# GpSimd's two sample-state transfers and its zeroes wait for four input units of block 1 instead of the last unit of block 0

## The chip, the cores and the metric

The kernel runs as one program on one core of a Trainium2 chip. The metric is the device time of one execution in microseconds (us), lower is better. Five queues of instructions run side by side: TensorE (PE in the rows; PEld is its weight load), VectorE (DVE), ScalarE (ACT), GpSimd (POOL) and SyncE (SP). Each takes its own instructions strictly in order, and they meet at counting semaphores. DMA engines move data; SyncE, ScalarE and GpSimd issue the transfers.

## The reference, cut to what matters

One inference step of a two-layer decoder, for a prompt of 512 tokens and for 8 samples of one token each, 520 tokens together (`TOK`), 1024 features. Layer 0 (block 0) is sparse attention, layer 1 (block 1) a sliding window of 128 keys; each is followed by an MLP with squared ReLU, and each half by a layer norm:

```python
for i in range(DEPTH):                       # DEPTH = 2
    m_p, ... = mixer_a_prompt / mixer_b_prompt (y_p, ...)
    m_s, ... = mixer_a_sample / mixer_b_sample (y_s, ...)
    y_p = post_norm(y_p, m_p, ...);  y_s = post_norm(y_s, m_s, ...)
    y_p = post_norm(y_p, squared_relu_mlp(y_p, w1, w2), ...)   # y_s alike
```

The part that the change touches is the window mixer of the samples. Its keys and values are a stored state of 128 tokens with the new token appended, and the last 128 of them are also outputs:

```python
keys = jnp.concatenate([win_k, k], axis=1)
vals = jnp.concatenate([win_v, v], axis=1)
...
return out @ w_out, keys[:, -wb:], vals[:, -wb:]
```

## The kernel before, in words

**Units.** Every dense product is cut into units: a 1024x128 block of weights (512 KB in `WRAW`) against all 520 tokens. A unit is 48 matmuls of 128x260: 8 contraction tiles, two token halves (`g`), and three products, because weights and activations are each split into a high and a low part. Units are counted over the whole program: block 1's input projection is units `B_IN` = 86 to 95, its output projection 96 to 103, then its MLP. `unit_done` counts finished units.

For each unit SyncE loads the raw weights (L432), ScalarE makes the high part (L1069 or L1019, `hi_done`), VectorE the low part as raw minus high (L1494 or L1419, `lo_dve`), and TensorE multiplies. There are two raw buffers, so the load of unit u+2 waits for VectorE's low part of unit u.

**End of block 0.** The last units of the MLP (`last_units`) run in halves of 260 tokens, and the layer norm of one half runs on VectorE and ScalarE while TensorE works on the other. VectorE writes the new activations `X32` by `even` (L1582) and their low parts `XL` (L1592). TensorE then takes the first four input units of block 1, 86 to 89, together in `first_quad` (matmuls on L606): half g=0 of all four in four steps of two tiles as `XL` comes, then `stats` for the other half, then half g=1. Unit 86 is counted only with its g=1 part, so `unit_done` reaches 90 when all of `first_quad` is done.

**Input projection.** Behind `first_quad` TensorE runs units 90 and 91, five transposes, and units 92 to 95 (`input_units(3, 5)`, L576). VectorE's program there, in order, is:

```python
low_parts(2, 3)                    # low parts of units 92, 93
dve.wait_ge(ev_act, A_OUT + 1)
dve.wait_ge(win_in, 32)
V.tensor_copy(KW[:, :, P:P + 1], ...)      # L2014
low_parts(3, 5)                    # low parts of units 94 to 97
```

TensorE begins unit 94 only with VectorE's low part of unit 94.

**GpSimd's part.** `KW` (keys, 128 partitions x 8 samples x 129) and `VW` (values, 127 rows x 8 samples x 128) receive the stored state. GpSimd waits for `unit_done`, issues the `KW` transfer (L555) and the `VW` transfer (L556), each of which adds 16 to `win_in`, clears `QB` (L559, `z_qb`), waits for the new values in `NAT` (`vt_ev`), and issues eight row transfers into `VW` (L562, `vwin_in`). `KW` and `QB` lie over `HL`, the low part of the MLP's hidden layer, which TensorE reads up to unit 85. The readers are: the copy on L2014 (`win_in`); the copies into `QB` on L2022 (`z_qb`) ahead of the attention; and TensorE inside block 1's attention (L988, L998).

Of the kernel before, what the change touches and what calls it, by code (L numbers as in the profile page):

```python
# [48 lines left out]
A_IN, A_OUT, MLP0, B_IN, B_OUT, MLP1, U_END = 0, 14, 22, 86, 96, 104, 168  # L49
# [124 lines left out]
def program(nc, io):  # L174
    with ExitStack() as ctx:
# [14 lines left out]
        def sem(name):  # L190
            return ctx.enter_context(nc.semaphore(name))
# [131 lines left out]
        unit_done = sem("unit_done")  # L323
# [59 lines left out]
        def load_page(eng, n, pg):  # L383

            fetch_page(eng, n, pg, page_number(eng, n, pg))

        def load_index_page(eng, half, c, pg, done):


            page = eng.value_load(PT[0:1, bass.ds(c * 16 + (8 * half + pg), 1)],  # L390
                                  min_val=0, max_val=POOL_PAGES - 1)
            eng.dma_start(IK[HD * half:HD * half + HD, bass.ds(c, 1), pg * P:(pg + 1) * P],  # L392
                          io["cacheI"][bass.ds(page, 1), :, :].rearrange("o d k -> d o k")
                          ).then_inc(done, 16)

        def page_numbers(eng, q, samples):

            return {n: [page_number(eng, n, pg) for pg in range(*kv_pages(n)[q])]
                    for n in samples}
# [6 lines left out]
        def load_values(eng, q, numbers):  # L406

            eng.wait_ge(unit_done, A_OUT)
            for n in V_LATE:
                if kv_before(n):  # L410
                    eng.wait_ge(kv_used, kv_before(n))
                load_sample(eng, q, n, numbers)
# [103 lines left out]
        @block.gpsimd  # L516
        def _(pool):
            nc.gpsimd.memset(NAT[:, 4, :], 0.0).then_inc(z_nat, 1)
            nc.gpsimd.memset(QB[:], 0.0).then_inc(z_qb, 1)
            pool.wait_ge(pt_in, 16)  # L520
            for half in range(2):
                with pool.Fori(0, 4 - half * IDX_SP) as c:
                    for pg in range(NPG):
                        load_index_page(pool, half, c, pg, idx_in)

            def low_part(u, slot):
                pool.wait_ge(hi_done, u + 1)
                nc.gpsimd.tensor_tensor(WLO[:, slot], WRAW[:, slot], WHI[:, slot].bitcast(F32),
                                        ALU.subtract).then_inc(lo_pool, 1)


            for n in (6, 7):
                with pool.Fori(0, NPG) as pg:
                    load_page(pool, n, pg)
            numbers = page_numbers(pool, 1, V_LATE)
            pool.wait_ge(ds_mm, 3)
            nc.gpsimd.memset(QB[:], 0.0).then_inc(z_qb, 1)
            with pool.Fori(0, 4) as pg:
                load_page(pool, 3, pg)
            for u in range(POOL_LO[0], A_OUT):  # L540
                low_part(u, u % 2)
                if u < POOL_LO[0] + 4:
                    load_page(pool, 3, 4 + u - POOL_LO[0])
            load_values(pool, 1, numbers)
            for u in range(A_OUT, POOL_LO[1]):
                low_part(u, u % 2)

            pool.wait_ge(ev_dve, 16)
            for h in range(NH):
                nc.gpsimd.tensor_tensor(BT[:, h, 256:512], BT[:, h, 256:512],  # L550
                                        CST[:, C_WIN:C_WIN + 2 * P], ALU.add
                                        ).then_inc(bwin, 1)

            pool.wait_ge(unit_done, B_IN)
            pool.dma_start(KW[:, :, 0:P], io["swk"]).then_inc(win_in, 16)  # L555
            pool.dma_start(VW[0:P - 1, :, :],  # L556
                           io["swv"][:, 1:P, :].rearrange("b k d -> k b d")
                           ).then_inc(win_in, 16)
            nc.gpsimd.memset(QB[:, 0:DB * 144], 0.0).then_inc(z_qb, 1)  # L559
            pool.wait_ge(vt_ev, 5)  # L560
            for b in range(DB):
                pool.dma_start(VW[P - 1:P, b, :], NAT[b:b + 1, 4, 0:P]  # L562
                               ).then_inc(vwin_in, 16)
# [1568 lines left out]
```

## Time and profile before

| | us |
|---|---|
| median of 3 runs | 1273.05 (1267.76 to 1275.14) |
| the profiled execution | 1270.1 |
| its span, first to last instruction | 1268.4 |
| TensorE busy | 1206.0 (95%) |
| VectorE busy | 708.6 (56%) |
| ScalarE busy | 473.9 (37%) |
| GpSimd busy | 94.8 (7%) |

Times below are microseconds from the start of the span. A timeline row is: start, duration, engine, line, operation, written tile <- read tiles, shape, and in brackets the idle time of the engine just before it with what ended it. TensorE's matmuls are pipelined: one has a duration of 0.28 us, but one starts every 0.12 us. The granted clock is TensorE's, as a share of full speed (2.4 GHz). The time that a transfer takes to land is counted from the start of its issue. The change touches the stretch from 690 to 780.

### The profile page before, as it was taken

Reading aid. Unit: us, or ns where it says so; the run is one execution under the profiler, and the core shown is the slowest. Engines: PE = TensorE matmul, PEld = TensorE weight load, DVE = VectorE, ACT = ScalarE, POOL = GpSimd, SP = SyncE. Lnnn points to the kernel's source line nnn. Section 1 sums busy time; section 2 is a strip of 40 time slices with the busy share of each in tenths; the row PEclk is TensorE's granted clock in tenths of the full one; section 3 lists DMA queues with packets and bytes.
Section 4 is the critical chain, followed back from the end, with each engine's and each line's share of the span. In section 5 each row is a group of like instructions: output and inputs, shape, how many; then the busy total and the mean of one; then the engine's idle time right before and its main releaser. Section 6 shows DMA issues by size and latency. Waiting matters only on the chain.

```text
span 1268.4 us, 25585 instructions
## 1 busy us (share of the span) xinstructions
PE 1206.0 (95%) x9574; PEld 1108.6 (87%) x9574; DVE 708.6 (56%) x1443; ACT 473.9 (37%) x865; POOL 94.8 (7%) x129
## 2 busy tenths in 40 slices
PE   8998979999999999999999897899999999999995
PEld 4958745589999999999999895599999999999995
DVE  2288989857843433433467627867633433433477
ACT  2342147744522331322334337834522322322332
POOL 4334300100040000000000210000000000000000
PEclk9999979999999999999999997999999999999998
DMA  6687570233122222222233221031222222222221
GB/s 202 192 282 242 182 240 16 75 111 103 48 91 92 96 86 97 86 93 89 93 110 114 50 93 48 1 101 67 67 84 100 83 100 83 98 84 98 84 84 68
DMA packets 62091, 131.04 MB, mean 103 GB/s; under 512 B 9739, under 2 KB 34483, under 8 KB 61890
## 3 DMA queue, kind: packets, MB, share of 16 engines
q1 hardware_dynamic: 44114, 112.94, 26.8%
q10 hardware_dynamic: 12096, 9.44, 2.4%
q0 software_dynamic: 5808, 7.67, 2.1%
q8 instruction: 48, 0.79, 0.3%
q14 instruction: 25, 0.20, 0.1%
HBM read 125.41 MB, written 9.79 MB: 107 GB/s over the span
## 4 chain that ended last, share of the span: by engine, by line
PE 72%; DVE 13%; issue 6%; POOLq 3%; ACT 2%; POOL 2%; SPq 1%; DMA 1%; ACTq 0%; DVEq 0%
PE PS L576 60%; PE PS L606 6%; DVE PB L1712 2%; DVE YA L1576 2%; PE PS L756 1%; PE PS L743 1%; DVE PB L1737 1%; SPq L379 1%; DVE YA L1563 1%; POOLq L370 1%; PE PS L770 1%; DVE X L1582 1%; DVE RSTD L1568 1%; POOL IK L392 1%; POOLq L390 1%
## 5 line engine op out<-in xcount | busy, mean ns | idle before, releaser
L1419 DVE TENSOR_TENSOR WLO<-WRAW,WHI 128x1024 fp32r<-128x1024 f32 x118 | 145.3, 1232 | 354.6 <-ACT WHI L1019 354.5
L1019 ACT ACTIVATE WHI<-WRAW 128x1024 fp32r<-128x1024 f32 x126 | 133.5, 1059 | 384.7 <-PE PS L576 363.0
L576 PE MATMUL PS<-XH,WHI 128*128 128x260 f32 x1344 | 273.4, 285 | 1.9 <-DVE XL L1744 1.6
L576 PE MATMUL PS<-XH,WLO 128*128 128x260 f32 x1344 | 270.7, 283 | 0.0
L576 PE MATMUL PS<-XL,WHI 128*128 128x260 f32 x1344 | 270.3, 283 | 0.0
L576 PEld LDWEIGHTS PS<-XH,WHI 128*128 128x128 f32 x1344 | 207.1, 188 | 7.9 <-issue 5.4
L576 PEld LDWEIGHTS PS<-XH,WLO 128*128 128x128 f32 x1344 | 207.1, 188 | 0.0
L576 PEld LDWEIGHTS PS<-XL,WHI 128*128 128x128 f32 x1344 | 206.7, 188 | 0.0
L576 PE MATMUL PS<-HH,WHI 128*128 128x260 f32 x896 | 181.4, 283 | 0.2 <-DVE HL L1443 0.2
L576 PE MATMUL PS<-HH,WLO 128*128 128x260 f32 x896 | 180.6, 283 | 0.0
L576 PE MATMUL PS<-HL,WHI 128*128 128x260 f32 x896 | 180.3, 283 | 0.0
L576 PEld LDWEIGHTS PS<-HH,WHI 128*128 128x128 f32 x896 | 138.2, 188 | 0.8 <-DVE HL L1443 0.4
L576 PEld LDWEIGHTS PS<-HH,WLO 128*128 128x128 f32 x896 | 138.1, 188 | 0.0
L576 PEld LDWEIGHTS PS<-HL,WHI 128*128 128x128 f32 x896 | 137.8, 188 | 0.0
L1030 ACT ACTIVATE HH<-S 128x520 f32 (+1 forms) x64 | 40.9, 640 | 105.2 <-DVE S L1438 105.2
L1443 DVE TENSOR_TENSOR HL<-S,HH 128x520 f32 (+1 forms) x64 | 45.3, 707 | 58.3 <-ACT HH L1030 58.3
L1186 ACT ACTIVATE PB<-PB,NMX 128x256 f32<-128x256 f32 (+3 forms) x128 | 64.9, 510 | 4.0 <-DVE NMX L1725 4.0
L756 PEld LDWEIGHTS PS<-CST,PB 128*128 128x128 f32 x272 | 30.9, 147 | 34.3 <-DVE PB L1737 31.5
L1712 DVE CUSTOM_DVE_ANT_0 PB<-PS,BT 128x256 f32<-128x256 f32 (+3 forms) x128 | 49.0, 437 | 14.3 <-PE PS L743 14.0
L756 PE MATMUL PS<-CST,PB 128*128 128x128 f32 x272 | 39.6, 290 | 15.3 <-DVE PB L1737 15.3
L1438 DVE TENSOR_TENSOR S<-RL,PS 128x520 f32<-128x520 f32 x64 | 44.6, 696 | 8.4 <-DVE WLO L1419 3.2
L1199 ACT ACTIVATE PTB<-PS 128x1024 f32<-128x1024 f32 (+1 forms) x36 | 35.2, 977 | 29.8 <-PE PS L756 29.8
(269 smaller groups left out, 1706.3 us busy)
## 6 DMA issues: line engine op xcount, KB each, us to landing
WRAW<-wall SPq DMA_DIRECT2D x168, 512.0 KB, 3.2
bias_skewed<-bias_seq SPq DMA_DIRECT2D x4, 1280.0 KB, 17.9
X<-xT SPq DMA_DIRECT2D x4, 520.0 KB, 6.5
X<-xT SPq DMA_DIRECT2D x1, 2080.0 KB, 11.4
yT<-X SPq DMA_DIRECT2D x8, 260.0 KB
KVB<-cacheK SPq DMA_DIRECT2D x16, 128.0 KB, 2.8
KVX<-cacheK SPq DMA_DIRECT2D x16, 128.0 KB, 3.0
KVB<-cacheK POOLq DMA_DIRECT2D x16, 128.0 KB, 6.8
```

The source lines that it names most:

```text
L576: mm = pe.matmul(PS[:, 2 * slot + g, 0:TG], w[:, slot, k, :], x[:, k, TG * g:TG * g + TG], start=(k == 0 and w is WHI and x is hi), stop=( ...
L606: mm = pe.matmul(PS[:, bank, 0:TG], w[:, k, :], x[:, k, TG * g:TG * g + TG], start=(k == 0 and parts == (hi, lo) and x is hi), stop=(k == ...
L756: mm = pe.transpose(PSF[:, 2048 + o:2048 + o + P], PB[:, i % 3, o:o + P], ident)
L1019: nc.scalar.activation(WHI[:, slot], WRAW[:, slot], ACT.Copy).then_inc(hi_done, 1)
L1030: nc.scalar.activation(HH[:, bass.ds(m, 1), :], S32[:].rearrange("p (o t) -> p o t", o=1), ACT.Copy).then_inc(hh_done, 1)
L1186: ins = nc.scalar.activation(x, x, ACT.Exp, bias=NMX[:, i % 3, j:j + 1], accum_out=SM[:, i % 3, j:j + 1])
L1199: nc.scalar.activation(PTB[:, i % 2, :].rearrange("p (e w) -> p e w", e=2)[:, :, 0:w], PS[:, 4:6, 0:w], ACT.Copy).then_inc(pt_ev, 1)
L1419: V.tensor_tensor(WLO[:, slot], WRAW[:, slot], WHI[:, slot].bitcast(F32), ALU.subtract).then_inc(lo_dve, 1)
L1438: V.tensor_tensor(S32[:].rearrange("p (g t) -> p g t", g=2), RL[:].rearrange("p (g t) -> p g t", g=2), src, ALU.mult).then_inc(ev_dve, 1)
L1443: V.tensor_tensor(HL[:, m, :], S32[:].rearrange("p (o t) -> p o t", o=1), HH[:, m, :].bitcast(F32), ALU.subtract).then_inc(hl_done, 1)
L1576: V.tensor_tensor(y, y, r, ALU.mult).then_inc(scaled, 1)
L1712: ins = V.tensor_tensor_reduce(out=PB[:, i % 3, at:at + w], in0=PSF[:, lg:lg + w], in1=add, scale=1.0, scalar=TAKEN, op0=ALU.add, op1=ALU.max,
```

## The change

One number: the count that GpSimd awaits before its block of transfers and zeroes. `B_IN` = 86 means that units 0 to 85 are done, `B_IN + 4` = 90 that units 86 to 89 are done too. No instruction is added, removed or moved within its engine.

```diff
@@ -551,7 +551,7 @@
-            pool.wait_ge(unit_done, B_IN)
+            pool.wait_ge(unit_done, B_IN + 4)
             pool.dma_start(KW[:, :, 0:P], io["swk"]).then_inc(win_in, 16)
             pool.dma_start(VW[0:P - 1, :, :],
                            io["swv"][:, 1:P, :].rearrange("b k d -> k b d")
                            ).then_inc(win_in, 16)
             nc.gpsimd.memset(QB[:, 0:DB * 144], 0.0).then_inc(z_qb, 1)
```

## Rows read from the trace of the kernel before

**Rows 1.** The page: busy time, share of the span and instructions of each engine.
```profile
PE 1206.0 (95%) x9574; PEld 1108.6 (87%) x9574; DVE 708.6 (56%) x1443; ACT 473.9 (37%) x865; POOL 94.8 (7%) x129
```

**Rows 2.** Timeline of GpSimd from 690 on, all its instructions.
```profile
690.18 0.92 POOL L555 DMA_DIRECT2D KW<-swk  x1 [309.78 <-PE PS L606]
696.39 6.71 POOL L556 DMA_DIRECT2D VW<-swv  x1 [5.28 <-issue]
703.10 1.09 POOL L559 MEMSET QB<- 128x1152 f32 x1
735.56 3.89 POOL L562 DMA_DIRECT2D VW<-NAT  x8 [31.38 <-ACT NAT L1368]
```

**Rows 3.** Timeline of VectorE around GpSimd's VW issue.
```profile
695.32 0.41 DVE L1582 TENSOR_SCALAR X<-YA,LNP 128x260 f32<-128x260 f32 x1
...
696.38 0.70 DVE L1576 TENSOR_TENSOR YA<-YA,RSTD 128x520 f32<-128x520 f32 x1
697.00 0.69 DVE L1592 TENSOR_TENSOR XL<-X,XH 128x520 fp32r<-128x520 f32 x1
697.61 5.59 DVE L1582 TENSOR_SCALAR X<-YA,LNP 128x260 f32<-128x260 f32 x1
703.12 0.41 DVE L1555 TENSOR_TENSOR RSTD<-PS,SQA 128x260 f32<-128x260 f32 x1
```

**Rows 4.** The chain that ended last, in order of time: start, us, what.
```profile
697.69 5.50 DVE X L1582
703.19 0.33 DVE RSTD L1555
...
709.62 11.74 PE PS L606 x96
721.36 11.52 PE PS L576 x96
732.88 0.44 PE PS L975 x4
733.32 0.11 PE PS L976
733.43 23.05 PE PS L576 x192
```

**Rows 5.** Timeline of TensorE (matmuls) in the second half of `first_quad`.
```profile
700.61 0.28 PE L606 MATMUL PS<-XH,WK 128*128 128x260 f32 x1
704.80 0.58 PE L606 MATMUL PS<-XH,WBT 128*128 128x260 f32 x1 [3.90 <-DVE XL L1592]
...
709.62 0.39 PE L606 MATMUL PS<-XH,WBT 128*128 128x260 f32 x1 [0.37 <-DVE XL L1592]
```

**Rows 6.** Stretches: length, busy per engine (instructions), granted clock, DMA share, GB/s.
```profile
704.80:709.25 4.45, 4.45 (x24) 4.25 (x24) 4.35 (x6) 1.50 (x3) 0.00 (x0) 0.67 0.19 26
706.00:707.00 1.00, 1.00 (x7) 1.00 (x6) 0.97 (x2) 0.00 (x0) 0.00 (x0) 0.50 0.19 25
708.00:708.50 0.50, 0.50 (x7) 0.50 (x5) 0.47 (x2) 0.50 (x1) 0.00 (x0) 1.00 0.20 29
```

**Rows 7.** DMA issues of 684 to 724: count, KB each, median us to landing.
```profile
KW<-swk POOLq DMA_DIRECT2D x1, 512.0 KB, 4.8
VW<-swv POOLq DMA_DIRECT2D x1, 508.0 KB, 37.9
```

**Rows 8.** DMA packets of 705 to 708: totals, and GpSimd's queue with its share of 16 engines.
```profile
DMA packets 415, 0.08 MB, mean 26 GB/s; under 512 B 399, under 2 KB 399, under 8 KB 415
...
q0 software_dynamic: 415, 0.08, 18.7%
```

**Rows 9.** The same for 723 to 726; q1 is SyncE's queue.
```profile
DMA packets 19, 0.09 MB, mean 29 GB/s; under 512 B 1, under 2 KB 1, under 8 KB 18
...
q0 software_dynamic: 9, 0.04, 3.6%
q1 hardware_dynamic: 9, 0.03, 2.9%
```

**Rows 10.** Weight loads on L432: issues with first and last start, of 712-720 and 720-740.
```profile
L432 SPq DMA_DIRECT2D WRAW<-wall x2: 332/332/333, 717.5 to 718.7; - x2
...
L432 SPq DMA_DIRECT2D WRAW<-wall x2: 333/333/333, 730.1 to 735.9; - x2
```

**Rows 11.** Timeline of VectorE in the input projection, all its instructions of 728 to 742.
```profile
728.73 1.23 DVE L1419 TENSOR_TENSOR WLO<-WRAW,WHI 128x1024 fp32r<-128x1024 f32 x1 [10.25 <-ACT WHI L1019]
734.50 1.23 DVE L1419 TENSOR_TENSOR WLO<-WRAW,WHI 128x1024 fp32r<-128x1024 f32 x1 [4.55 <-ACT WHI L1019]
735.65 0.17 DVE L2014 COPY KW<-UQ 128x8 f32<-128x8 f32 x1
740.88 1.23 DVE L1419 TENSOR_TENSOR WLO<-WRAW,WHI 128x1024 fp32r<-128x1024 f32 x1 [5.07 <-ACT WHI L1019]
```

**Rows 12.** The later readers: VectorE's copy into QB, and TensorE's use of VW.
```profile
759.33 0.43 DVE L2022 COPY QB<-UQ 64x64 f32<-64x64 f32 x2
...
L998 PE MATMUL PS<-PTD,VW x16: 182/263/263, 778.0 to 779.6; 128*128 128x16 f32 x16
```

## The prediction, made before the changed kernel was run

> **What bounds the kernel now.** I read the busy shares first: TensorE is busy for 95% of the span [rows 1], so a change elsewhere counts only where it makes TensorE wait or stop waiting. GpSimd has four entries behind 690 [rows 2]; I went through them one by one, asking who was disturbed and who waited.
>
> The chain of waits then shows something odd: a step of 5.50 us of VectorE on L1582 [rows 4]. The timeline of VectorE gives the reason [rows 3]. The same instruction with the same shape took 0.41 us at 695.32 and 5.59 us at 697.61. It ended at 703.2, and GpSimd's issue of the `VW` transfer ran from 696.39 to 703.10 [rows 2]. Two tensor-tensor instructions inside the issue, at 696.38 and 697.00, took their usual 0.70 and 0.69 us [rows 3]. So the issue holds up this one form of VectorE instruction until it is over. TensorE stood idle for 3.90 us for the `XL` behind it, and the restart ran at clock 0.50 before it came back to 1.00 [rows 5, 6].
>
> That is what the old place of the block costs. The new place has to be judged by the second thing the rows show: the `VW` transfer took 37.9 us from its issue to its landing, against 4.8 us for the equally large `KW` [rows 7]. It landed at 696.39 + 37.9 = 734.3. VectorE's copy on L2014, which waits for it, ran at 735.65, directly behind a low part [rows 11]. The landing was in time by 735.65 - 734.3 = 1.35 us. There is nothing to spare for a later start.
>
> **Part 1, the stall that goes.** The block leaves the layer norm. L1582 falls from 5.59 back to 0.41: 5.18 us. ScalarE and VectorE have nothing else late there, as the chain passes through this instruction and on through VectorE to 709.62 [rows 4]. TensorE's last matmul before the gap started at 700.61 [rows 5]; with `XL` 5.2 us earlier it does not wait there at all, and the half-clock restart goes too, but neither adds to the gain, since the 96 matmuls from 709.62 on waited for VectorE [rows 4, 5]. Everything from 704 on comes 5.2 us earlier: a gain of 5.2 us as seen at 721.36, the end of `first_quad`.
>
> **Part 2, where the block goes.** `unit_done` reaches 90 when the 96 matmuls end, at 721.36 in old time [rows 4], that is 716.2 in new time. The old release was at 690.18 [rows 2]. With the same durations [rows 2]: `KW` issued at 716.3, `VW` issued from 716.3 + 6.2 = 722.5 to 729.2, zeroes until 730.3. Within 722.5 to 729.2 VectorE has one instruction, the low part of unit 92 (728.73 before, 723.5 now [rows 11]). It is a tensor-tensor, the form that ran undisturbed before [rows 3], so I price it at nothing. If it were held until 729.2, unit 92 would start about 2 us late, and the longer wait below would swallow that.
>
> **Part 3, when VW lands now.** It took 734.3 - 703.1 = 31.2 us behind the end of its issue. In a stretch with no weight load GpSimd's queue moved 415 - 399 = 16 large packets in 3 us, 0.19 us each [rows 8]. The data is 127 rows of 4 KB, so alone it takes 127 x 0.19 = 24 us, with 0.9 us of start-up (packets begin at about 704.0) some 25 us. Beside a weight load the weight queue had 9 packets and this queue 9 in 3 us, with 6.5% of 16 engines busy [rows 9]: that is one engine taking turns. Three weight loads fell within the 31.2 us, issued at 717.5, 718.7 and 730.1 [rows 10], so one costs about (31.2 - 25)/3 = 2.1 us. In the new place one load falls within it, the one from 735.9, now 730.7 [rows 10]; the next waits for a low part that VectorE isn't free to make. So the landing is at 729.2 + 25 + 2 = 756. The bounds: no collision 754, the full old duration 760.4.
>
> **The rule beside the row.** The Trainium skill, DMA: Bandwidth & Descriptors, "Why a DMA increments its semaphore by 16 and not by 1", says that a transfer is split over the largest k up to 16 that divides both outer sizes, so 127 partitions go to one engine, but that some copies issued by GpSimd are spread over all 16 all the same. By the first half the sum stands as above; the second half is a rival below.
>
> **Part 4, the wait that is added.** VectorE reaches `win_in` behind the low part of unit 93, at 735.65 - 5.2 = 730.5 in new time, and stands until 756. Queued behind it are the copy and the low parts of units 94 to 97. TensorE does units 92 and 93 (48 x 0.12 = 5.76 us each) and begins unit 94 at 733.43 + 11.52 = 744.95 in old time [rows 4], 739.8 in new. Now it needs 756.1 + 0.15 (copy) + 1.23 (low part [rows 11]) = 757.5. TensorE is idle for 17.7 us. Against the old 744.95 unit 94 starts 12.5 us late; this already has the 5.2 us gain in it.
>
> **Part 5, the restart.** After the 3.90 us gap 24 matmuls took 4.45 us, at a mean clock of 0.67 [rows 6], where at full clock they take 24 x 0.12 = 2.9 us: 1.5 us lost. The new gap is longer; I take the same 1.5 us for it, from nothing (below which the clock can't help) to 5.8 us, a whole unit at half clock.
>
> Nothing else becomes late. Loads of units 96 and 97 move with VectorE and have a unit of TensorE time each as cover. The zeroes end at 730.3 and are read at 759.33 + 14. The eight row transfers wait for `NAT` as before, at 735.56 - 5.2 = 730.4, when GpSimd is just free; they may land behind `VW`, near 758, and are wanted at 778.0 + 14 [rows 12]: 34 us of cover.
>
> **Sum:** 12.5 + 1.5 = 14 us slower. On the profiled execution that gives 1270.1 + 14 = 1284.1, on the median 1273.05 + 14 = 1287.1. The four times shown, 1267.76 to 1275.14, don't tell which is the typical one; I take 1286. The bounds of the landing are 2 us down and 4.3 us up, those of the clock 1.5 down and 4.3 up.
>
> **Rivals.**
> - **Faster: VW lands in time.** Only the landing matters. If it comes by 757.5 - 17.7 - 1.4 = 738.4, 9.2 us behind the issue's end, unit 94 doesn't wait and the 5.2 us are kept: 1273 - 5.2 = 1268. For it speaks `KW`, which has the same bytes and lands in 4.8 us [rows 7]. Against it: the same transfer, with the same shape, took 31.2 us behind its issue here, at 0.19 us a packet when alone [rows 8]. By the skill's exception of 16 engines it would land like `KW`; the trace shows one engine [rows 9]. 6%.
> - **Slower still: 20 to 27 us.** If TensorE stays at clock 0.50 for a unit or more behind the long gap, and `VW` needs its full 31.2 us or more: 18.3 - 1.4 + 5.8 is near 23 us, 1296. The clock was back after 3 us [rows 6], which speaks against it. 7%.
> - **Nothing happens.** If GpSimd's wait for unit 86 were not what released it, the change would do nothing: 1273. But the row says that a TensorE matmul on L606 ended its idle time of 309.78 us [rows 2]. With gain and loss cancelling by accident, 3%.
>
> **How the numbers follow.** The forecast, a landing between 754 and 761, has 84%. Slower by over 0.5% (6.4 us, about what a measurement of this kernel can tell from no change) is the forecast and the heavier rival, 91%; the same 3%; faster by over 0.5% has part of the first rival, whose 5.2 us are just under that line, and I give it 2%, the other 4% going to the same, 7% in all. The range: the forecast with its bounds, 14 - 3.5 to 14 + 7, on a base of 1270 to 1273: 1280 to 1294. That leaves out most of the rivals.
>
> **What the changed profile should show.** L1582 at 0.41 us throughout the layer norm; no TensorE gap of 3.9 us in `first_quad`; `KW` issued near 716 and `VW` near 722.5; no VectorE instruction lengthened in 722 to 729; `VW` landing 33 to 38 us from its issue, near 756; VectorE idle from 730.5 until then in front of L2014; one TensorE gap of 17 to 22 us before unit 94, with a low part L1419 as its end and a restart at half clock; behind that, the same program 14 us later. The prediction is wrong if `VW` lands within 10 us of its issue's end, or if L2014 isn't followed by a late low part.

## The result, and the profile after

| | before | changed |
|---|---|---|
| median of 4 runs, us | 1274.1 (1267.76 to 1275.32) | 1291.58 (1285.45 to 1293.0) |
| the profiled execution, us | 1270.1 | 1285.45 |
| its span, us | 1268.4 | 1283.7 |
| TensorE busy, us | 1206.0 | 1202.6 |

The ratio is 1.0143, with a 95% interval of 1.0118 to 1.0167: the change makes the kernel slower by about 18 us (17.5 by the medians). TensorE is busy for about as long as before, so what was added is waiting. The waits of TensorE name it in one line (engine, line, what it waited for: us in total, times, longest):

```profile
PE PS L576 <- DVE WLO L1419: 20.9, 1, 20.9
PE PS L756 <- DVE PB L1737: 16.0, 21, 4.0
...
PE PS L606 <- DVE XL L1592: 3.3, 6, 0.8
```

The first line is new. The last is what is left of the wait of 3.90 us in `first_quad` [rows 5]. GpSimd, to be read against [rows 2]:

```profile
715.44 0.92 POOL L555 DMA_DIRECT2D KW<-swk  x1 [336.18 <-PE PS L606]
721.57 6.71 POOL L556 DMA_DIRECT2D VW<-swv  x1 [5.21 <-issue]
728.27 1.08 POOL L559 MEMSET QB<- 128x1152 f32 x1
729.34 1.51 POOL L562 DMA_DIRECT2D VW<-NAT  x3
758.27 2.38 POOL L562 DMA_DIRECT2D VW<-NAT  x5 [27.42 <-issue]
```

The timeline of VectorE, first in the layer norm (against [rows 3]), then in the input projection (against [rows 11]):

```profile
694.16 0.41 DVE L1582 TENSOR_SCALAR X<-YA,LNP 128x260 f32<-128x260 f32 x1
...
695.83 0.69 DVE L1592 TENSOR_TENSOR XL<-X,XH 128x520 fp32r<-128x520 f32 x1
696.44 0.41 DVE L1582 TENSOR_SCALAR X<-YA,LNP 128x260 f32<-128x260 f32 x1
696.86 0.43 DVE L1555 TENSOR_TENSOR RSTD<-PS,SQA 128x260 f32<-128x260 f32 x1
...
722.50 1.23 DVE L1419 TENSOR_TENSOR WLO<-WRAW,WHI 128x1024 fp32r<-128x1024 f32 x1 [10.27 <-ACT WHI L1019]
728.28 1.23 DVE L1419 TENSOR_TENSOR WLO<-WRAW,WHI 128x1024 fp32r<-128x1024 f32 x1 [4.55 <-ACT WHI L1019]
758.05 0.17 DVE L2014 COPY KW<-UQ 128x8 f32<-128x8 f32 x1 [28.54 <-DMA VW<-swv]
758.26 2.36 DVE L1419 TENSOR_TENSOR WLO<-WRAW,WHI 128x1024 fp32r<-128x1024 f32 x2
```

The instruction on L1582 that took 5.59 us takes 0.41. The low part at 722.50, inside GpSimd's `VW` issue (721.57 to 728.27), takes its usual 1.23 us. Then VectorE stands for 28.54 us in front of the copy, until `VW` has landed, and the low parts of units 94 and 95 come behind it. The chain that ended last now runs through the transfer (start, us, what):

```profile
703.39 11.76 PE PS L606 x96
...
715.44 0.92 POOL KW L555
716.36 5.21 issue
721.57 36.39 DMA VW<-swv
...
758.26 1.24 DVE WLO L1419
...
759.62 13.36 PE PS L576 x96
```

The 96 matmuls of units 94 and 95 take 13.36 us. Before, the 192 of units 92 to 95 took 23.05 [rows 4], so 11.5 for 96. The stretch after the restart shows the clock (columns as in rows 6):

```profile
759.62:762.20 2.58, 2.58 (x12) 2.58 (x13) 1.00 (x1) 0.00 (x0) 1.03 (x3) 0.50 0.61 189
763.00:766.00 3.00, 3.00 (x27) 3.00 (x26) 0.00 (x0) 0.00 (x0) 0.00 (x0) 0.97 0.36 142
```

**The sum in the two traces.** The changed execution was already 1.16 us ahead at 695 (L1582 at 695.32 [rows 3] and at 694.16), for reasons ahead of the change, so I count from there. The end of `first_quad` is at 721.36 and at 703.39 + 11.76 = 715.15: 6.21 - 1.16 = 5.05 us gained. Unit 94 starts at 744.95 and at 759.62: 14.67 + 1.16 = 15.8 us late. The restart costs 13.36 - 11.5 = 1.8 more, 17.6 in all at the end of the projection. TensorE's use of `VW` on L998 begins at 778.0 [rows 12] and, in the changed kernel, at 792.9: 16.1 us late. So 1.5 us came back at the start of the attention, and the spans differ by 1283.7 - 1268.4 + 1.16 = 16.5 us.

**The 1.5 us are luck.** In both traces TensorE's granted clock falls to 0.50 in the first stretch of the attention: for 10.2 us before (from 765.8 to 776.0), for 3.4 us in the changed trace (from 783.7 to 787.1). From the first attention matmul to the use of `VW` they take 20.7 and 19.1 us. The experiments below show that this length changes whatever the place of the block: 3.4 us of half clock in the two with `VW` on a count of its own (19.4 and 19.2 us in all), 6.8 us in four others (20.0 to 20.4), and 10.2 us with the split rows at the old place (20.8). So these two profiled executions show the loss about 1.5 us too small; 17.6 us is what the change cost, and the medians (17.5) agree.

### The profile page after: what moved, and what is told of

It is laid out like the page before. It is cut to its first block, busy times and chain, and to the rows that moved or that the text cites. A ratio compares the mean times of both kernels' runs of the same rounds, so it can differ in the third digit from the quotient of the medians.

```text
span 1283.7 us, 25585 instructions
## 1 busy us (share of the span) xinstructions
PE 1202.6 (94%) x9574; PEld 1108.2 (86%) x9574; DVE 703.3 (55%) x1443; ACT 473.8 (37%) x865; POOL 94.9 (7%) x129
## 4 chain that ended last, share of the span: by engine, by line
PE 69%; DVE 12%; issue 6%; DMA 4%; POOLq 3%; ACT 3%; POOL 2%; SPq 1%; ACTq 0%; DVEq 0%
PE PS L576 58%; PE PS L606 6%; DMA VW<-swv 3%; DVE PB L1712 2%; DVE YA L1576 2%; DVE PB L1737 1%; SPq L379 1%; PE PS L743 1%; DVE YA L1563 1%; PE PS L756 1%; POOLq L370 1%; PE PS L770 1%; DVE RSTD L1568 1%; POOL IK L392 1%; POOLq L390 1%
## 5 line engine op out<-in xcount | busy, mean ns | idle before, releaser
L576 PE MATMUL PS<-XH,WHI 128*128 128x260 f32 x1344 | 274.9, 286 | 22.8 <-DVE WLO L1419 20.9
L756 PE MATMUL PS<-CST,PB 128*128 128x128 f32 x272 | 38.4, 284 | 16.1 <-DVE PB L1737 16.0
```

The source lines that it names most:

```text
L576: mm = pe.matmul(PS[:, 2 * slot + g, 0:TG], w[:, slot, k, :], x[:, k, TG * g:TG * g + TG], start=(k == 0 and w is WHI and x is hi), stop=( ...
L756: mm = pe.transpose(PSF[:, 2048 + o:2048 + o + P], PB[:, i % 3, o:o + P], ident)
```

## The experiments

Two theories were set against each other. The **landing theory**: the gain in the layer norm is real, and the loss is VectorE's stand in front of the copy until `VW` lands. The **place theory**: the block disturbs its new place whatever is waited for, or the old stall was hidden and its end gains nothing. A second pair asked why `VW` is slow: because its 127 rows all go through **one DMA engine**, or because of its small pieces and GpSimd as issuer. The ratios are to the kernel before, on the same chip.

### VW on a count of its own, at the new place

```diff
 pool.wait_ge(unit_done, B_IN + 4)
 ...
-               ).then_inc(win_in, 16)          # VW
+               ).then_inc(vwin_in, 16)
 # VectorE's copy, TensorE (L985) and ScalarE (L1397)
-wait_ge(win_in, 32)
+wait_ge(win_in, 16)
 # TensorE (L996) and ScalarE (L1396)
-wait_ge(vwin_in, 16 * DB)
+wait_ge(vwin_in, 16 * (DB + 1))
```

> The changed kernel, but the VW transfer counts on the semaphore of the row transfers, so VectorE's copy waits for KW alone. Landing theory (the loss is VectorE standing in front of the copy until VW lands, and the stall of L1582 is a real 5.2 us gain): VectorE idle in front of L2014 falls from 28.5 us to nothing, the TensorE gap of 20.9 us before unit 94 goes, VW still lands 33 to 36 us after its issue; time 5 us below the kernel before, ratio 0.996. Rival 1 (the block disturbs its new place whatever is waited for, by its issue or by the weight loads beside it): slower than before, near 1.01. Rival 2 (the stall in the layer norm was hidden anyway): ratio 1.000.

Ratio 0.9951 (0.9933 to 0.9969), median 1265.56 us against 1271.22. VectorE and GpSimd in its timeline:

```profile
725.67 6.71 POOL L556 DMA_DIRECT2D VW<-swv  x1 [5.25 <-issue]
...
769.48 2.39 POOL L562 DMA_DIRECT2D VW<-NAT  x5 [34.57 <-issue]
```

```profile
732.35 1.23 DVE L1419 TENSOR_TENSOR WLO<-WRAW,WHI 128x1024 fp32r<-128x1024 f32 x1 [4.55 <-ACT WHI L1019]
733.49 0.17 DVE L2014 COPY KW<-UQ 128x8 f32<-128x8 f32 x1
738.72 1.23 DVE L1419 TENSOR_TENSOR WLO<-WRAW,WHI 128x1024 fp32r<-128x1024 f32 x1 [5.07 <-ACT WHI L1019]
```

The block sits where the changed kernel has it, and the whole loss is gone; what is left is the gain of the layer norm. The place theory falls on both counts. One expectation was missed: `VW` did not land in 33 to 36 us. The profile gives its landing as 23.5 us, which can't be right, as packets of 4 KB still left GpSimd's queue until 768. That is 42 us from the start of the issue, beside five weight loads, where VectorE's stand let only one through in the changed kernel. The last row transfers were issued from 769.48 to 771.87, and TensorE read `VW` at 774.5: this version has 2.6 us left for them to land, where 1.5 to 3 us is what such a transfer took, so almost no cover.

### The same count at the old place

The same edits with `pool.wait_ge(unit_done, B_IN)`.

> The kernel before, with VW on its own count as in the run beside it, and the block at its old place (86 units). Landing theory: VW landed 1.35 us ahead of the copy anyway, so nothing changes, ratio 1.000, and L1582 is still lengthened to about 5.6 us. If the own count alone brings the gain, the ratio is near 0.996 and the layer-norm stall isn't what is won.

Ratio 1.0 (0.9982 to 1.0018). The stall is there as before, and it ends at 702.60, where the `VW` issue ended at 702.50:

```profile
694.68 0.41 DVE L1582 TENSOR_SCALAR X<-YA,LNP 128x260 f32<-128x260 f32 x1
...
696.96 5.64 DVE L1582 TENSOR_SCALAR X<-YA,LNP 128x260 f32<-128x260 f32 x1
```

So the count alone gains nothing, and between this run and the one above lies the new place with its landing uncovered: 0.5%. That is what the change would have brought had nobody waited for `VW`.

### VW as 112 and 15 rows, at the new place

```diff
 pool.wait_ge(unit_done, B_IN + 4)
 pool.dma_start(KW[:, :, 0:P], io["swk"]).then_inc(win_in, 16)
-pool.dma_start(VW[0:P - 1, :, :],
-               io["swv"][:, 1:P, :].rearrange("b k d -> k b d")
-               ).then_inc(win_in, 16)
+for r0, r1 in ((0, 112), (112, P - 1)):
+    pool.dma_start(VW[r0:r1, :, :],
+                   io["swv"][:, r0 + 1:r1 + 1, :].rearrange("b k d -> k b d")
+                   ).then_inc(win_in, 16)
 ...
-wait_ge(win_in, 32)
+wait_ge(win_in, 48)
```

> The changed kernel with one edit: the 127 rows of VW are sent as 112 rows and 15 rows, the copy waits for both. One-engine theory (127 rows go through one DMA engine because of their number): the two land within 5 to 8 us of the issue's end, by 738, TensorE's gap of 20.9 us goes, time 5 us below the kernel before, ratio 0.996. Rival (the transfer is slow because it is 512-byte pieces issued by GpSimd, whatever the rows): still about 30 us, time as the changed kernel, ratio 1.014.

Ratio 0.9953 (0.9935 to 0.9971). Here everybody waits for `VW` as in the changed kernel, and it costs nothing. GpSimd's timeline (the kernel is one line longer here, so lines behind 556 shift by one), and the DMA issues with the median us to landing:

```profile
716.12 0.92 POOL L555 DMA_DIRECT2D KW<-swk  x1 [336.12 <-PE PS L607]
717.03 1.45 POOL L557 DMA_DIRECT2D VW<-swv  x2
718.46 1.10 POOL L560 MEMSET QB<- 128x1152 f32 x1
730.00 3.89 POOL L563 DMA_DIRECT2D VW<-NAT  x8 [10.44 <-ACT NAT L1369]
```

```profile
VW<-swv POOLq DMA_DIRECT2D x1, 448.0 KB, 5.6
...
VW<-swv POOLq DMA_DIRECT2D x1, 60.0 KB, 5.4
```

Same bytes, same pieces, same issuer: the landing falls from 36.4 to 5.6 us. GpSimd's queue kept 87.8% of the 16 engines busy from 719 to 722.5; in the changed kernel, in a stretch with no other traffic (750 to 753), it was 6.3%, which is one engine of 16. Earlier in its flight, as in [rows 8], the share was higher: some 1,900 packets under 512 B went out beside the large ones, against 60 with 112 and 15 rows. What they are for is not shown; they did not slow the large ones, of which 15 or 16 went in 3 us with them and without. It is the number of rows that made the landing late. By the Trainium skill, DMA: Bandwidth & Descriptors, "Why a DMA increments its semaphore by 16 and not by 1", a transfer uses the largest number of engines up to 16 that divides the outer sizes of both its sides; that makes 1 for 127, 16 for 112, 15 for 15. The two traces agree with that part of the page, by these shares; its exception, that some GpSimd copies are spread over 16 whatever their rows, did not occur here. Three more things went with the 127 that I had not tied to it: the issue falls from 6.71 us to 1.45 for two, the 5.2 us between the `KW` and the `VW` issue are gone, and the eight row transfers go out in one piece.

### VW as 112 and 15 rows, at the old place

The same edits with `pool.wait_ge(unit_done, B_IN)`.

> The kernel before with the block at its old place (86 units), and only the 127 rows of VW sent as 112 and 15. In the run with the split at the new place the two issues took 1.45 us together instead of 6.71. If the stall of L1582 lasts as long as GpSimd's issue does, it shrinks to 1.5 us or less or misses the instruction altogether, and this kernel gains the same 5 us as the changed place: ratio 0.996. If the stall comes from issuing there at all, whatever its length, L1582 stays near 5.6 us and the ratio is 1.000.

Ratio 0.9966 (0.9952 to 0.9981). The issues ran from 693.27 to 694.72, and the stretch of VectorE around them has no lengthened instruction:

```profile
693.27 1.45 POOL L557 DMA_DIRECT2D VW<-swv  x2
```

```profile
692.69 1.23 DVE L1495 TENSOR_TENSOR WK<-WRAW,WK 128x1024 fp32r<-128x1024 f32 x1
693.83 0.69 DVE L1593 TENSOR_TENSOR XL<-X,XH 128x520 fp32r<-128x520 f32 x1
694.44 0.42 DVE L1527 TENSOR_TENSOR YA<-YA,PS 128x260 f32<-128x260 f32 x1
...
697.50 0.42 DVE L1583 TENSOR_SCALAR X<-YA,LNP 128x260 f32<-128x260 f32 x1
```

There was no tensor-scalar instruction within those 1.45 us, so the stall missed, and nobody had to move the block. What a short issue does to a tensor-scalar instruction that it meets was not tried. Both troubles, the stall and the late landing, came with the shape of one transfer and went with it.

### Two and six input units instead of four

`pool.wait_ge(unit_done, B_IN + 2)` and `B_IN + 6`, nothing else.

> The block waits for two input units (count 88) instead of four, everything else as in the changed kernel. These two units finish 24 matmuls, 2.9 us, before the four. Landing theory: release, landing of VW and TensorE's gap all 3 us less than in the changed kernel, gap near 18 us, ratio near 1.012, L1582 at 0.41 us. Rival (a fixed cost of the new place): as the changed kernel, gap 20.9 us.

> The block waits for six input units (count 92) instead of four. Landing theory: the release comes two units, 11.5 us, later than in the changed kernel, and everything from the copy on with it: VW lands near 769.5, TensorE's gap grows from 20.9 to about 32 us, time 11.5 us above the changed kernel, about 1303, ratio 1.023. Rival (a fixed cost of the new place): time as the changed kernel, 1.014.

| count | ratio to before | release, us from a common point, less that with four units | start of the VW issue, alike | flight of VW behind its issue's end, us | landing, alike | TensorE's gap, us |
|---|---|---|---|---|---|---|
| B_IN + 2 | 1.0141 (1.012 to 1.0161) | -2.9 | -1.5 | 29.0 | -2.2 | 18.7 |
| B_IN + 4 | 1.0143 (1.0118 to 1.0167) | 0 | 0 | 29.7 | 0 | 20.9 |
| B_IN + 6 | 1.0183 (1.016 to 1.0206) | +11.5 | +11.4 | 27.2 | +8.9 | 29.9 |

The common point is the second half-tile of the layer norm (L1582 at 684.65, 685.70 and 690.47). The releases are as expected to 0.1 us. TensorE's gap changes by -2.2 and +9.0 us, just as the landing does, so there is no fixed cost of the place. The landing does not follow the release one to one, for two reasons. With two units, the `VW` issue began 6.54 us behind the end of the `KW` issue instead of 5.21, and `KW` took 6.0 us to land instead of 4.7: in all six traces with the 127 rows behind `KW`, the `VW` issue began 1.4 to 1.5 us after `KW` had landed. With six units, SyncE's next load was already waiting for VectorE when the issue ended, and `VW` had DMA to itself: 27.2 us. The whole times show six units as the slowest, by an interval that just overlaps that of four, and between two and four they show no difference. For six units the expected gap of about 32 us and the 1303 us were too high (29.9, and 1295.88).

### VW far ahead

```diff
+pool.dma_start(VW[0:P - 1, :, :], ...).then_inc(vwin_in, 16)   # 127 rows, as before
 pool.wait_ge(unit_done, B_IN)
 pool.dma_start(KW[:, :, 0:P], io["swk"]).then_inc(win_in, 16)
-pool.dma_start(VW[0:P - 1, :, :], ...).then_inc(win_in, 16)
 nc.gpsimd.memset(QB[:, 0:DB * 144], 0.0).then_inc(z_qb, 1)
```

The waits are those of the version with `VW` on a count of its own.

> VW (127 rows in one transfer, its own count) is issued far ahead, behind GpSimd's last work of block 0's MLP near 380 us, where its place in memory is free; KW and the zeroes stay at the old place. If the stall of L1582 belongs to the VW issue alone, L1582 is 0.41 us throughout and the time is 5 us below the kernel before, ratio 0.996. If the KW issue or the zeroes stall VectorE there too, L1582 or a neighbour is lengthened again and the ratio is near 1.000. The one-engine transfer now runs beside the MLP's weight loads: if these become late for TensorE, up to some us of the gain are lost again.

Ratio 0.9963 (0.9949 to 0.9978). GpSimd's rows, with the zeroes now directly behind the `KW` issue, and VectorE's beside them:

```profile
382.51 6.74 POOL L554 DMA_DIRECT2D VW<-swv  x1
692.45 0.90 POOL L558 DMA_DIRECT2D KW<-swk  x1 [303.20 <-PE PS L606]
693.35 1.08 POOL L559 MEMSET QB<- 128x1152 f32 x1
```

```profile
692.66 1.23 DVE L1494 TENSOR_TENSOR WK<-WRAW,WK 128x1024 fp32r<-128x1024 f32 x1
693.81 0.69 DVE L1592 TENSOR_TENSOR XL<-X,XH 128x520 fp32r<-128x520 f32 x1
...
697.47 0.41 DVE L1582 TENSOR_SCALAR X<-YA,LNP 128x260 f32<-128x260 f32 x1
```

L1582 is 0.41 or 0.42 us throughout and the 5 us are gained, so the stall went with the `VW` issue. That is weaker than it looks as a statement on the other two: the `KW` issue and the zeroes (692.45 to 694.43) met only tensor-tensor instructions, and so did the `VW` issue at its new time (a low part and a scalar-tensor-tensor instruction, 1.23 and 0.69 us as usual). That the `KW` issue or the zeroes would spare a tensor-scalar instruction is not shown. The slow transfer beside the MLP made the weight loads of 385 to 420 land in 8.2 us instead of 3.2, and TensorE still had no gap there: it was busy for 20.00 of the 20 us from 400 on, in both kernels. That price was feared and didn't come.

## Why the prediction was right

- **The stall (part 1)** was read rightly: 5.2 us forecast, 5.05 measured, and 0.5% of the whole time in the run that takes the landing away from the copy.
- **The new place (part 2)**: the release at 716.2 and the `VW` issue from 722.5 to 729.2 were forecast; counted from the common 695 they came at 716.6 and from 722.7 to 729.4. The low part inside the issue was undisturbed, as the form of the instruction said.
- **The landing (part 3)** is the term that was mis-sized: 27 us behind the issue's end, measured 29.7. It was made of 25 us alone and 2.1 us for the one weight load met. The run with six units shows it alone: 27.2 us, which also puts the lower bound of 754 for a landing without collision some 2 us too early. The 127 packets take 0.20 us each (15 in each free stretch of 3 us of the changed trace), about 25 us, and another 2 us lie around them; I had 24 and 0.9. What the neighbours cost is not a constant: (31.2 - 27.2)/3 = 1.3 us for each of the three loads of the kernel before, and 2.5 us in the changed kernel for one load and two output transfers of 64 KB from ScalarE's queue. I split 31.2 us wrongly into an own part and a neighbours' part, and that showed as soon as the number of loads changed.
- **The added wait (part 4)**: unit 94 came 15.8 us late instead of 12.5, of which the flight of `VW` is 2.7 us. The rest is 0.2 us of a later issue and 0.3 us between the landing and the first matmul (1.66 us, where copy and low part had been put at 1.4).
- **The restart (part 5)**: 1.8 us against 1.5. A gap of 20.9 us cost hardly more than the gap of 3.90 us had: the clock was at 0.50 for some 3.4 us of matmuls and then full.
- **The sum**: 14 us forecast, 17.6 at the end of the projection, 16.5 at the end of the span (with 1.5 us of luck in the clock), 17.5 by the medians. Of the 5.6 us between the forecast of 1286 and the 1291.58 measured, 3.5 are the change; the other 2.1 are the base, as the kernel before has 1274.1 and not the 1272 on which I had settled.
- **The rivals**: a landing in time is what the 112 and 15 rows produce, and then the kernel is indeed faster than before, by 0.3 to 0.65%; the page's exception that would have produced it with 127 rows is excluded here. A half clock lasting a whole unit did not occur behind the gap.

What remains open is what makes the half clock in the attention last 3.4, 6.8 or 10.2 us, and whether the stall of L1582 needs a long issue.

The best versions here are the ones with `VW` in 112 and 15 rows, at either place (0.9953 and 0.9966, whose intervals overlap). They also have more cover than the version with two counts.

## What to carry to other kernels

Before a transfer is moved later, find the first wait that its landing has to meet, on every engine, and compare the landing from the trace with that wait: here the landing had 1.35 us to spare, and the release was moved by 26. When two transfers of nearly equal size land in 4.8 and 37.9 us, look at the number of rows first; cutting 127 into 112 and 15 removed the late landing and the long issue, and the shorter issue no longer met the instruction that had stalled. And when a duration is split into its own part and what it shares with others, get the own part from a stretch without the others, since only that part moves along unchanged. Last, a run in which a suspect meets nothing that it could disturb does not clear it.

## What the runs showed of the hardware that was not expected

- GpSimd's issue of a transfer was itself long for the 127-row shape: 6.71 us, against 1.45 us for two transfers with 112 and 15 rows.
- GpSimd waited between transfers when 127 rows were among them. The `VW` issue began only 1.4 to 1.5 us after `KW` had landed; with 112 and 15 rows it followed the `KW` issue at once. And tiny transfers behind it were held back: in the changed kernel three of eight row transfers were issued from 729.34, and the other five only at 758.27, 0.3 us after `VW` had landed (25.2 and 25.0 us of waiting with two and six units). With 112 and 15 rows all eight went in 3.89 us. The break behind the third is not `VW`'s alone, though: it also stood, 2.84 us long, in the version with the count alone at the old place, where `VW` had landed 1.7 us before the first row transfer.
- The `VW` issue stretched a VectorE tensor-scalar instruction (0.41 to 5.59 us, and 5.64 in a second run) and left tensor-tensor instructions alone, even a low part of 1.23 us wholly inside it. The Trainium skill, SBUF — State Buffer, "SBUF: two separate sides", describes a port pair that VectorE's two-port instructions and GpSimd hold exclusively, each blocking the other until its instruction ends; the stall ended within 0.1 us of the issue's end in both runs, which fits that rule. The port itself is seen in no run here.
- One DMA engine with the slow transfer on it slowed the weight loads beside it: 8.2 us instead of 3.2 in the MLP, 8.6 us for the one load in the changed kernel. In the MLP TensorE had no gap by it.
